# Half of the first modulation slabs multiplied by TensorE instead of VectorE

## The chip, the cores and the metric

The kernel runs on one core of a Trainium2 chip. The metric is the device time of one execution in microseconds; the kernel before takes 1960.63 us, the median of three runs from 1959.63 to 1964.99. All work is in float32. Matrix products that carry the weight are made of three products of split operands (high and low parts), but the products of this change are plain float32.

## The reference

Two transformer blocks in a row on a sequence of 256 positions of width 1024. The first begins with a modulation vector, which is what the change touches:

```python
c_act = jax.nn.silu(c)                       # 1 x 1024
mod = c_act @ w_ada[l] + b_ada[l]            # 1024 x 9216
sh1, sc1, g1, sh2, sc2, g2, sh3, sc3, g3 = [m[:, None, :] for m in jnp.split(mod, N_MOD, axis=-1)]
u = _modulate(_rmsnorm(h, norm_ffn1[l]), sh1, sc1)
h = h + 0.5 * g1 * _swiglu(u, w_ffn1_up[l], w_ffn1_down[l])
```

Everything after that (a gated delta mixer, a second feed-forward part, then the second block) is the same in both kernels. The first feed-forward part needs `sh1` and `sc1`, the first 2048 columns of `mod`, before its first matrix product can start.

## The kernel before, in words

All weights come through one ring of four buffers, `raw`, each of 128 partitions x 8 depth blocks x 256 columns of float32: 1 MB, a slab. SyncE issues each slab as two loads of 512 KB. The ring is governed by one counter, `raw_used`: it starts at 4, and the load of slab r waits until it has reached r + 1. Every consumer of a slab adds one when it is done, so slab r + 4 is loaded when slab r is free. `raw_full` of the buffer says that a slab has landed.

`w_ada` has 36 slabs, each of 256 columns of `mod`. Eight (`UPFRONT`) stand ahead of everything and give `sh1` and `sc1`. 14 more stand between the slabs of the first up-projection (`up1a`), 14 stand later.

A modulation slab is a product of one row with a 1024 x 256 matrix. VectorE does it in `dve_ada`: for each of the 8 depth blocks it multiplies the 128 x 256 block by the scalar `c_act` of each partition and adds it to one of two running sums (line 499 for the first two blocks, line 502 for the other six), then adds the two (line 505, which adds one to `raw_used`). What is left is a sum over the 128 partitions, which TensorE does in `pe_ada` (line 511): for each half of 128 columns the sum is the stationary operand and a column of ones streams past it, and the result is one column of bank 7. `ada_sum` counts these results (it starts at 2); VectorE may begin slab a when it has reached a + 1, because `acc` has two places in turn.

The opening is one block, in which the engines do this, in the order written:

- SyncE issues the loads up to the fifth slab behind the eight.
- ScalarE squares `h` for the first norm (line 615) and makes the high part of the first up-projection slab, `w_hi` (line 389).
- VectorE does the eight slabs, adds the bias in `dve_mod` (line 520, the row `mod`), which waits for all sums, and makes the low part, `w_lo` (line 397).
- TensorE sums the squares over the partitions in `total` (line 621), then does `pe_ada` eight times.

A barrier ends the block. Behind it the next block starts with `scale_col` (line 672), the norm, and the up-projection, in which every pair of columns takes one slab of `w_ffn1_up` and, up to pair 14, one of `w_ada`.

Of the kernel before, what the change touches and what calls it, by code (L numbers as in the profile page):

```python
# [23 lines left out]
P = 128  # L24
# [10 lines left out]
SLAB_K = 8  # L35
SLAB_N = 256
RING = 4
LANDED = 32
# [11 lines left out]
def at(i, step, base):  # L50

    return base if i is None else i * step + base
# [125 lines left out]
def build(nc, t, const_np, place):  # L178
    with ExitStack() as ctx:
        def sb(name, shape, dt=F32, c=ctx):  # L180
            return c.enter_context(nc.sbuf_tensor(name, shape, dt))
# [3 lines left out]
        def sem(name):  # L185
            s = nc.alloc_semaphore(name=name)
            stage_sems.append(s)
            return s
# [18 lines left out]
        raw = sb("raw", [P, RING, SLAB_K, SLAB_N])  # L207
# [11 lines left out]
        c_act = sb("c_act", [P, DT])  # L219
        banks = [ctx.enter_context(nc.psum_tensor(f"bank{i}", [P, 512], F32)) for i in range(8)]  # L220

        def const(name, rows=P):
            a, b = place[name]
            return cst[0:rows, a:b]
# [9 lines left out]
        def col(name, i, n=1):  # L234
            v, row = vcol[name]
            return vec[:, v, row + i:row + i + n]


        raw_full = [sem(f"raw_full{i}") for i in range(RING)]
        raw_used = sem("raw_used")  # L240
# [5 lines left out]
        ada_step = sem("ada_step")  # L246
        ada_sum = sem("ada_sum")
# [3 lines left out]
        def link(eng, who, ins):  # L251

            steps[who] += 1
            ins.then_inc(step[who], 1)
            eng.wait_ge(step[who], steps[who])
# [27 lines left out]
        UPFRONT, BESIDE_UP = 8, 14  # L283
# [48 lines left out]
        def load_to(sp, end):  # L332


            end = min(end, len(plan.raw))
            r = issued[0]
            while r < end:
                def rate(lap):

                    out = []  # L340
                    for u in range(RING):
                        a, b = plan.raw[r + lap * RING + u], plan.raw[r + (lap + 1) * RING + u]
                        if a[0] is not b[0] or a[2] != b[2]:
                            return None
                        out.append(b[1] - a[1])
                    return out
                laps, first = 1, rate(0) if r + 2 * RING <= end else None
                if first:
                    while r + (laps + 1) * RING <= end and rate(laps - 1) == first:
                        laps += 1  # L350
                if first and laps >= 2:
                    with sp.Fori(0, laps, 1) as i:
                        for u in range(RING):
                            sec, n, g = plan.raw[r + u]

                            sp.wait_ge(raw_used, i * RING + (r + u + 1))
                            load(sp, r + u, sec, i * first[u] + n, g)
                    r += laps * RING
                else:
                    sec, n, g = plan.raw[r]  # L360
                    sp.wait_ge(raw_used, r + 1)
                    load(sp, r, sec, n, g)
                    r += 1
            issued[0] = max(end, issued[0])

        def numbers(sec, i, U, u, g):

            k = u * sec.g + g
            r, s = sec.r0 + k * sec.rs, sec.s0 + k
            return (at(i, U * sec.g * sec.rs, r), r, at(i, U * sec.g, s), s,  # L370
                    at(i, LANDED * U * sec.g * sec.rs // RING, LANDED * (r // RING + 1)))
# [19 lines left out]
        def split_lo(dve, nxt):  # L391
            if nxt is None:
                return
            sec, g, (r, r_at, s, s_at, landed) = nxt
            kt = sec.kts[g]
            dve.wait_ge(hi_done, s + 1)
            nc.vector.tensor_tensor(w_lo[:, s_at % 2, 0:kt], raw[:, r_at % RING, 0:kt],  # L397
                                    w_hi[:, s_at % 2, 0:kt].bitcast(F32), ALU.subtract).then_inc(raw_used, 1)
# [84 lines left out]
        acc = sb("acc", [P, 3, SLAB_N])  # L483
        ADA_STEPS = SLAB_K

        def dve_ada(dve, a, a_at, r, r_at, landed, k0=0, k1=SLAB_K):

            if k0 == 0:  # L490
                dve.wait_ge(raw_full[r_at % RING], landed)
                dve.wait_ge(ada_sum, a + 1)
            for k in range(k0, k1):
                src, w = raw[:, r_at % RING, k], c_act[:, k:k + 1]
                part = acc[:, 2 if k % 2 else a_at % 2]
                if k == 1:
                    dve.wait_ge(raw_used, r + RING)
                if k < 2:
                    nc.vector.tensor_scalar(part, src, w, None, ALU.mult).then_inc(ada_step, 1)
                else:  # L500
                    dve.wait_ge(ada_step, a * ADA_STEPS + (k - 1))
                    nc.vector.scalar_tensor_tensor(out=part, in0=src, scalar=w, in1=part, op0=ALU.mult, op1=ALU.add).then_inc(ada_step, 1)  # L502
            if k1 == SLAB_K:
                dve.wait_ge(ada_step, a * ADA_STEPS + ADA_STEPS)
                nc.vector.tensor_tensor(acc[:, a_at % 2], acc[:, a_at % 2], acc[:, 2], ALU.add).then_inc(raw_used, 1)

        def pe_ada(pe, r, a, a_at, col0):

            pe.wait_ge(raw_used, r + 1 + RING)
            for j in range(2):  # L510
                mm = nc.tensor.matmul(banks[7][:, col0 + j:col0 + j + 1] if isinstance(col0, int)
                                      else banks[7][:, bass.ds(col0 + j, 1)],
                                      acc[:, a_at % 2, j * P:(j + 1) * P], const("ones")[:, 0:1],
                                      start=True, stop=True)
            mm.then_inc(ada_sum, 1)

        def dve_mod(dve, a, b, sums):

            dve.wait_ge(ada_sum, sums + 2)
            link(dve, "dve", nc.vector.tensor_tensor(mod[:, a:b], banks[7][:, a:b], col("b_ada", a, b - a), ALU.add))  # L520
# [4 lines left out]
        start = ExitStack()  # L525
# [3 lines left out]
        with nc.Block() as block:  # L529
            @block.sync  # L530
            def _(sp):
                sp.dma_start(cst[:], t["const"]).then_inc(loaded[0], 16)
                for v, group in enumerate(VECTORS):
                    row = 0
                    for name, rows in group:
                        src = t[name]
                        src = (src.rearrange("a (r p) -> (a r) p", p=P) if len(src.shape) == 2 else
                               src.rearrange("(r p) -> r p", p=P) if len(src.shape) == 1 else
                               src.rearrange("a b (r p) -> (a b r) p", p=P) if src.shape[-1] % P == 0 else
                               src.rearrange("a (r b) p -> (a r) (b p)", b=2))  # L540
                        sp.dma_start(rows_v[row:row + rows, v], src).then_inc(loaded[1 + v], 16)
                        row += rows
                load_to(sp, RING)
# [138 lines left out]
        with nc.Block() as block:  # L682
            @block.sync
            def _(sp):
                load_to(sp, S["up1a"].r0 + 1 + RING)

            @block.scalar
            def _(act):
                for u in range(4):
                    norm_ffn1.square(act, u, sq0)  # L690
                split_hi(act, (S["up1a"], 0, numbers(S["up1a"], None, 0, 0, 0)))

            @block.vector
            def _(dve):
                for a in range(UPFRONT):
                    dve_ada(dve, a, a, a, a, LANDED * (a // RING + 1))
                dve_mod(dve, 0, 2 * UPFRONT, UPFRONT)
                split_lo(dve, (S["up1a"], 0, numbers(S["up1a"], None, 0, 0, 0)))

            @block.tensor  # L700
            def _(pe):
                for u in range(4):
                    norm_ffn1.total(pe, u, sq0)
                for a in range(UPFRONT):
                    pe_ada(pe, a, a, a, 2 * a)
        first_sq.close()

        p_zero, p_ready, p_done, xu_ready, x_done, yu_ready, y_done = (
# [5 lines left out]
        def swiglu(ups, down, gate, norm, then):  # L714
# [7 lines left out]
            with ExitStack() as c:  # L722
# [6 lines left out]
                with nc.Block() as block:  # L729
# [32 lines left out]
                    def _(dve):  # L762
# [3 lines left out]
                        def between(i, u, U):  # L766
                            a = at(i, U, u + UPFRONT)
                            r_at = ups[0].r0 + 2 * u + 1
                            landed = at(i, LANDED * 2 * U // RING, LANDED * (r_at // RING + 1))
                            dve_ada(dve, a, u + UPFRONT, at(i, 2 * U, r_at), r_at, landed)  # L770
# [1302 lines left out]
        a = {n: sem("a_" + n) for n in names}  # L2073
# [296 lines left out]
```

## Time and profile before

| | |
|---|---|
| median of three runs | 1960.63 us (1959.63 to 1964.99) |
| the profiled execution, its span | 1960.6 us |
| TensorE busy | 1681.0 us, 86% |
| VectorE busy | 1136.0 us, 58% |
| ScalarE busy | 756.5 us, 39% |
| read from HBM | 249.99 MB |

The span is from the first to the last instruction of the profiled execution, and there is nothing around it that the runs' times would add: it stands at their median. The shares are means over stages with different limits. The opening that the change touches is the first 50 us of the span. TensorE's rows come in pairs, a weight load (PEld) and a matmul (PE), which overlap; the granted clock (PEclk) is 1.00 at 2.4 GHz and 0.50 at 1.2 GHz.

### The profile page before, as it was taken

The page shows a single profiled execution, that of the slowest core. Times are in us where ns is not written, and L with a number is a line of the kernel's source. Part 1 is how long each engine was busy: PE and PEld are TensorE (multiplying, and loading weights), DVE is VectorE, ACT ScalarE, POOL GpSimd, SP SyncE. Part 2 cuts the span into 40 slices and gives each one's busy share as a digit, 9 for nine tenths or more (in the row PEclk, how much of TensorE's full clock was granted, in tenths as well). Part 3 has the DMA queues.
Part 4 walks back from the last instruction along what each step waited for, and adds up shares of the span by engine and source line. Part 5 has one row for each costly group of instructions (what it writes and reads, how often), then busy time and mean ns, then how long its engine had stood idle before and what let it go on. Part 6 is the DMA issues. An engine that isn't in the chain of part 4 may idle for free. (4 is left out here: it accounts for less than half of the span.)

```text
span 1960.6 us, 36564 instructions
## 1 busy us (share of the span) xinstructions
PE 1681.0 (86%) x15063; PEld 1586.5 (81%) x15063; DVE 1136.0 (58%) x1885; ACT 756.5 (39%) x1040; POOL 108.2 (6%) x139
## 2 busy tenths in 40 slices
PE   3899989958888988999886886789997979779997
PEld 3899989927878987999885774689997956579997
DVE  6895457968795555444466554554335358554334
ACT  1554345731003634554344000356433434446432
POOL 0011000002120000110000210000000020000000
PEclk7899989958999998999987985889998985789998
DMA  9897545402234354665451000245452510225451
GB/s 301 235 315 221 178 133 171 150 0 88 87 97 122 120 182 129 173 192 178 124 161 43 2 2 7 86 129 173 162 170 97 172 50 1 86 87 171 157 170 39
DMA packets 297020, 252.88 MB, mean 129 GB/s; under 512 B 9032, under 2 KB 295597, under 8 KB 296893
## 3 DMA queue, kind: packets, MB, share of 16 engines
q1 hardware_dynamic: 296589, 249.96, 41.2%
q8 instruction: 94, 1.54, 0.3%
q10 hardware_dynamic: 304, 1.11, 0.1%
q14 instruction: 33, 0.27, 0.0%
HBM read 249.99 MB, written 1.05 MB: 128 GB/s over the span
## 5 line engine op out<-in xcount | busy, mean ns | idle before, releaser
L397 DVE TENSOR_TENSOR w_lo<-raw,w_hi 128x2048 fp32r<-128x2048 f32 (+2 forms) x203 | 456.4, 2250 | 549.6 <-ACT w_hi L389 549.3
L464 PE MATMUL bank<-x_hi,w_hi 128*128 128x256 f32 (+1 forms) x2224 | 651.6, 293 | 71.9 <-DVE x_lo L658 41.6
L466 PE MATMUL bank<-x_hi,w_lo 128*128 128x256 f32 (+1 forms) x2224 | 642.6, 289 | 0.0
L465 PE MATMUL bank<-x_lo,w_hi 128*128 128x256 f32 (+1 forms) x2224 | 642.5, 289 | 0.0
L389 ACT ACTIVATE w_hi<-raw 128x2048 fp32r<-128x2048 f32 (+2 forms) x203 | 381.6, 1880 | 470.5 <-PE bank L466 432.9
L464 PEld LDWEIGHTS bank<-x_hi,w_hi 128*128 128x128 f32 x2224 | 428.6, 193 | 81.1 <-issue 68.3
L466 PEld LDWEIGHTS bank<-x_hi,w_lo 128*128 128x128 f32 x2224 | 430.0, 193 | 0.0
L465 PEld LDWEIGHTS bank<-x_lo,w_hi 128*128 128x128 f32 x2224 | 428.9, 193 | 0.9 <-issue 0.7
L464 PE MATMUL bank<-mh_hi,w_hi 128*128 128x272 f32 x512 | 150.5, 294 | 6.6 <-PEq L2014 6.6
L466 PE MATMUL bank<-mh_hi,w_lo 128*128 128x272 f32 x512 | 149.4, 292 | 0.0
L465 PE MATMUL bank<-mh_lo,w_hi 128*128 128x272 f32 x512 | 149.1, 291 | 0.0
L464 PEld LDWEIGHTS bank<-mh_hi,w_hi 128*128 128x128 f32 x512 | 97.8, 191 | 7.2 <-issue 7.0
L464 PE MATMUL bank<-hid_hi,w_hi 128*128 128x256 f32 x352 | 100.2, 285 | 0.4 <-DVE w_lo L397 0.4
L466 PE MATMUL bank<-hid_hi,w_lo 128*128 128x256 f32 x352 | 99.0, 281 | 0.0
L465 PE MATMUL bank<-hid_lo,w_hi 128*128 128x256 f32 x352 | 99.0, 281 | 0.0
L465 PEld LDWEIGHTS bank<-mh_lo,w_hi 128*128 128x128 f32 x512 | 97.9, 191 | 0.2
L466 PEld LDWEIGHTS bank<-mh_hi,w_lo 128*128 128x128 f32 x512 | 97.8, 191 | 0.0
L502 DVE SCALAR_TENSOR_TENSOR acc<-raw,c_act,acc 128x256 f32<-128x256 f32 x216 | 96.7, 504 | 0.1
L621 PE MATMUL bank<-sq,cst 128*128 128x272 f32 (+1 forms) x160 | 51.4, 467 | 21.8 <-ACT sq L615 21.8
L464 PEld LDWEIGHTS bank<-hid_hi,w_hi 128*128 128x128 f32 x352 | 66.3, 188 | 1.1 <-issue 0.8
L465 PEld LDWEIGHTS bank<-hid_lo,w_hi 128*128 128x128 f32 x352 | 66.3, 188 | 0.1
L466 PEld LDWEIGHTS bank<-hid_hi,w_lo 128*128 128x128 f32 x352 | 66.2, 188 | 0.0
(427 smaller groups left out, 2206.9 us busy)
## 6 DMA issues: line engine op xcount, KB each, us to landing
raw<-in_mlp_w SPq DMA_DIRECT2D x128, 512.0 KB, 4.3
raw<-in_w_ffn_up SPq DMA_DIRECT2D x88, 512.0 KB, 5.2
raw<-in_w_ada SPq DMA_DIRECT2D x72, 512.0 KB, 4.7
raw<-in_w_in SPq DMA_DIRECT2D x60, 512.0 KB, 4.6
raw<-in_w_ffn_down SPq DMA_DIRECT2D x32, 512.0 KB, 4.4
raw<-in_od_w_in SPq DMA_DIRECT2D x24, 512.0 KB, 4.4
raw<-in_ev_w_in SPq DMA_DIRECT2D x18, 512.0 KB, 4.6
raw<-in_w_ffn_down SPq DMA_DIRECT2D x16, 384.0 KB, 3.8
```

The costliest lines, as they stand in the source:

```text
L389: nc.scalar.activation(w_hi[:, s_at % 2, 0:kt], raw[:, r_at % RING, 0:kt], ACT.Copy).then_inc(hi_done, 1)
L397: nc.vector.tensor_tensor(w_lo[:, s_at % 2, 0:kt], raw[:, r_at % RING, 0:kt], w_hi[:, s_at % 2, 0:kt].bitcast(F32), ALU.subtract).then_inc ...
L464: nc.tensor.matmul(out, hi, xh[:, k0 + k, 0:L], start=start, stop=False)
L465: nc.tensor.matmul(out, hi, xl[:, k0 + k, 0:L], start=False, stop=False)
L466: mm = nc.tensor.matmul(out, lo, xh[:, k0 + k, 0:L], start=False, stop=stop)
L502: nc.vector.scalar_tensor_tensor(out=part, in0=src, scalar=w, in1=part, op0=ALU.mult, op1=ALU.add).then_inc(ada_step, 1)
L621: mm = nc.tensor.matmul(banks[6][:, 0:self.L], const("ones"), sq[:, k], start=k == 0, stop=k == DT - 1)
```

## The change

Of the eight slabs ahead, those with even numbers (0, 2, 4, 6) stay as they are. Those with odd numbers go to TensorE whole, in a new function, `pe_ada_whole`: for each half of 128 columns it runs over the 8 depth blocks, with the 128 x 128 weight block from `raw` as the stationary operand and one column of `c_act` streamed past it, and accumulates in one column of bank 7. That is 16 float32 matmuls for a slab.

TensorE's order is slab 1 whole, the sum of slab 0, slab 3 whole, the sum of slab 2, and so on. VectorE's order is slab 0, 2, 4, 6. As the ring's counter has to rise in the order of the slabs, VectorE adds the one for the odd slab: in the middle of the next even slab, before its seventh depth block, it waits until TensorE has summed both slabs before (`ada_sum` at a + 2), adds one to `raw_used`, and goes on. For slab 7 it does so after `mod`.

```diff
-        def dve_ada(dve, a, a_at, r, r_at, landed, k0=0, k1=SLAB_K):
+        def dve_ada(dve, a, a_at, r, r_at, landed, k0=0, k1=SLAB_K, since=0):
...
-                    dve.wait_ge(raw_used, r + RING)
+                    dve.wait_ge(raw_used, r + RING - since)
...
+        def pe_ada_whole(pe, r, landed, col0):
+
+            pe.wait_ge(raw_full[r % RING], landed)
+            for j in range(2):
+                for k in range(SLAB_K):
+                    mm = nc.tensor.matmul(banks[7][:, col0 + j:col0 + j + 1], raw[:, r % RING, k, j * P:(j + 1) * P], c_act[:, k:k + 1],
+                                          start=k == 0, stop=k == SLAB_K - 1)
+            mm.then_inc(ada_sum, 1)
...
             def _(dve):
-                for a in range(UPFRONT):
-                    dve_ada(dve, a, a, a, a, LANDED * (a // RING + 1))
+                for a in range(0, UPFRONT, 2):
+                    landed = LANDED * (a // RING + 1)
+                    if a:
+                        dve_ada(dve, a, a // 2, a, a, landed, 0, SLAB_K - 2, since=1)
+                        dve.wait_ge(ada_sum, a + 2)
+                        dve.sem_inc(raw_used, 1)
+                        dve_ada(dve, a, a // 2, a, a, landed, SLAB_K - 2, SLAB_K)
+                    else:
+                        dve_ada(dve, a, 0, a, a, landed)
+                    dve.sem_inc(ada_step, ADA_STEPS)
                 dve_mod(dve, 0, 2 * UPFRONT, UPFRONT)
+                dve.sem_inc(raw_used, 1)
                 split_lo(dve, (S["up1a"], 0, numbers(S["up1a"], None, 0, 0, 0)))
...
             def _(pe):
...
-                for a in range(UPFRONT):
-                    pe_ada(pe, a, a, a, 2 * a)
+                for a in range(0, UPFRONT, 2):
+                    pe_ada_whole(pe, a + 1, LANDED * ((a + 1) // RING + 1), 2 * a + 2)
+                    pe_ada(pe, a, a, a // 2, 2 * a)
```

The order of TensorE's instructions behind the norm's total, before the change; each row is an instruction of the program, with its output and inputs and what it waits for:

```order
L621 MATMUL bank6<-sq0,cst 128x256
L511 MATMUL bank7<-cst,acc 128x1 [waits raw_used]
L511 MATMUL bank7<-cst,acc 128x1
L511 MATMUL bank7<-cst,acc 128x1 [waits raw_used]
L511 MATMUL bank7<-cst,acc 128x1
L511 MATMUL bank7<-cst,acc 128x1 [waits raw_used]
L511 MATMUL bank7<-cst,acc 128x1
```

The same place of the changed kernel:

```order
L630 MATMUL bank6<-sq0,cst 128x256
L522 MATMUL bank7<-c_act,raw 128x1 [waits raw_full1]
L522 MATMUL bank7<-c_act,raw 128x1 x15
L511 MATMUL bank7<-cst,acc 128x1 [waits raw_used]
L511 MATMUL bank7<-cst,acc 128x1
L522 MATMUL bank7<-c_act,raw 128x1 [waits raw_full3]
L522 MATMUL bank7<-c_act,raw 128x1 x15
L511 MATMUL bank7<-cst,acc 128x1 [waits raw_used]
```

The two sums of a slab that VectorE made remain for every second slab, and ahead of them stand 16 matmuls that wait for a landed slab and not for VectorE.

VectorE's order before the change, from the second slab on:

```order
L499 TENSOR_SCALAR acc<-raw,c_act 128x256 [waits ada_sum,raw_full1]
L499 TENSOR_SCALAR acc<-raw,c_act 128x256 [waits raw_used]
L502 SCALAR_TENSOR_TENSOR acc<-raw,c_act,acc 128x256 [waits ada_step] x6
L505 TENSOR_TENSOR acc<-acc 128x256 [waits ada_step]
L499 TENSOR_SCALAR acc<-raw,c_act 128x256 [waits ada_sum,raw_full2]
```

The same place of the changed kernel, up to the start of slab 4:

```order
L499 TENSOR_SCALAR acc<-raw,c_act 128x256 [waits ada_sum,raw_full2]
L499 TENSOR_SCALAR acc<-raw,c_act 128x256 [waits raw_used]
L502 SCALAR_TENSOR_TENSOR acc<-raw,c_act,acc 128x256 [waits ada_step] x4
L502 SCALAR_TENSOR_TENSOR acc<-raw,c_act,acc 128x256 [waits ada_sum,ada_step]
L502 SCALAR_TENSOR_TENSOR acc<-raw,c_act,acc 128x256 [waits ada_step]
L505 TENSOR_TENSOR acc<-acc 128x256 [waits ada_step]
L499 TENSOR_SCALAR acc<-raw,c_act 128x256 [waits ada_sum,raw_full0]
```

Slabs 1, 3, 5 and 7 are gone from VectorE, and each slab left has a second wait for `ada_sum` in its middle.

## Rows read from the trace of the kernel before

**Rows 1.** Who waited for whom, 17 to 46.3 us: total, times, longest.
```profile
PE bank L511 <- DVE acc L505: 15.1, 6, 3.2
...
DVE mod L520 <- PE bank L511: 1.1, 1, 1.1
DVE acc L499 <- PE bank L511: 0.6, 1, 0.6
```

**Rows 2.** Timeline of VectorE and ScalarE: start, duration, instruction, [idle before, releaser].
```profile
17.09 0.62 DVE L499 TENSOR_SCALAR acc<-raw,c_act 128x256 f32<-128x256 f32 x2 [0.41 <-PEq L529]
17.62 2.46 DVE L502 SCALAR_TENSOR_TENSOR acc<-raw,c_act,acc 128x256 f32<-128x256 f32 x6
20.11 0.42 DVE L505 TENSOR_TENSOR acc<-acc 128x256 f32<-128x256 f32 x1
20.45 0.61 DVE L499 TENSOR_SCALAR acc<-raw,c_act 128x256 f32<-128x256 f32 x2
...
40.79 1.91 ACT L389 ACTIVATE w_hi<-raw 128x2048 fp32r<-128x2048 f32 x1 [21.62 <-DMA raw<-in_w_ffn_up]
44.51 0.42 DVE L505 TENSOR_TENSOR acc<-acc 128x256 f32<-128x256 f32 x1
46.04 0.17 DVE L520 TENSOR_TENSOR mod<-bank,vec 128x16 f32<-128x16 f32 x1 [1.10 <-PE bank L511]
46.24 2.29 DVE L397 TENSOR_TENSOR w_lo<-raw,w_hi 128x2048 fp32r<-128x2048 f32 x1
50.10 0.17 DVE L672 SCALAR_TENSOR_TENSOR scale_col<-mod,vec 128x8 f32<-128x8 f32 x1 [1.56 <-PEq L682]
```

**Rows 3.** TensorE: timeline from 17 us, then line 511's count and ns (min/median/max).
```profile
17.66 6.42 PE L621 MATMUL bank<-sq,cst 128*128 128x256 f32 x16 [1.31 <-ACT sq L615]
...
23.70 1.08 PEld L511 LDWEIGHTS bank<-cst,acc 128*128 128x128 f32 x8
...
L511 PE MATMUL bank<-cst,acc x4: 352/352/372, 28.0 to 28.7; 128*128 128x1 f32 x4
...
L511 PE MATMUL bank<-cst,acc x144: 166/250/373, 23.9 to 599.0; 128*128 128x1 f32 x144
```

**Rows 4.** Timeline of the weight loads of a run with 8 columns each.
```profile
400.25 0.55 PEld L1045 LDWEIGHTS bank<-g_log,cst 128*128 128x128 f32 x2
400.69 0.55 PEld L1044 LDWEIGHTS bank<-g_log,cst 128*128 128x128 f32 x2
...
402.82 0.55 PEld L1045 LDWEIGHTS bank<-g_log,cst 128*128 128x128 f32 x2
```

**Rows 5.** Timeline of the matmuls of a run with 32 columns each.
```profile
383.11 0.18 PE L985 MATMUL bank<-w_ba_hi,x_hi 128*128 128x32 f32 x1
...
384.03 0.26 PE L985 MATMUL bank<-w_ba_hi,x_hi 128*128 128x32 f32 x1
...
388.05 0.26 PE L985 MATMUL bank<-w_ba_hi,x_hi 128*128 128x32 f32 x1
...
388.50 0.63 PE L988 MATMUL bank<-heads_row,cst 1*128 1x32 f32 x2
```

**Rows 6.** Stretches: length, busy of PE, PEld, DVE, ACT, POOL, PEclk, DMA share, GB/s.
```profile
17.00:20.00 3.00, 2.34 (x6) 1.89 (x7) 2.91 (x8) 2.17 (x4) 0.00 (x0) 1.00 1.10 347
...
23.00:26.00 3.00, 1.86 (x13) 1.67 (x11) 2.34 (x8) 0.00 (x0) 0.00 (x0) 1.00 1.00 311
26.00:27.00 1.00, 0.00 (x0) 0.00 (x0) 1.00 (x3) 0.00 (x0) 0.00 (x0) 0.78 1.09 379
27.00:30.00 3.00, 1.01 (x4) 0.93 (x4) 2.96 (x9) 0.00 (x0) 0.00 (x0) 0.50 0.72 222
...
381.60:385.00 3.40, 3.40 (x33) 3.40 (x31) 3.40 (x9) 1.58 (x5) 0.00 (x0) 1.00 0.00 0
385.00:388.30 3.30, 3.30 (x32) 3.30 (x31) 3.27 (x9) 0.63 (x1) 0.00 (x0) 1.00 0.01 2
388.40:391.80 3.40, 0.73 (x4) 0.56 (x3) 1.23 (x1) 3.37 (x8) 0.00 (x0) 0.50 0.00 0
```

**Rows 7.** Loads of line 330: at 24.3 us, from 20 to 50, the first eight.
```profile
L330 SPq DMA_DIRECT2D raw<-in_w_ada x1: 508/508/508, 24.3 to 24.3; - x1
DMA to landing us min/median/max: 4.8/4.8/4.8
...
L330 SPq DMA_DIRECT2D raw<-in_w_ada x12: 367/435/509, 20.6 to 45.4; - x12
DMA to landing us min/median/max: 3.4/4.4/5.6
...
L330 SPq DMA_DIRECT2D raw<-in_w_ada x8: 409/510/1859, 8.6 to 14.2; - x8
DMA to landing us min/median/max: 3.6/7.5/9.2
```

**Rows 8.** The stretch behind the barrier, same columns as rows 6.
```profile
50.00:145.00 95.00, 84.55 (x670) 83.79 (x671) 89.23 (x162) 54.24 (x58) 8.34 (x11) 0.93 0.98 275
```

## The prediction, on record before the changed kernel ran

> **What bounds the kernel now.** I read first the two-engine picture of the opening (who waited for whom from 17 to 46 us), then the timelines of VectorE and TensorE there, then the clock by stretches, then the loads, and last the stage behind the barrier. The opening is a chain on VectorE. TensorE waits for VectorE's sum six times, 15.1 us in all, and VectorE, once started, waits for TensorE only twice, 0.6 us at the third slab and 1.1 us at the very end [rows 1]. A slab costs VectorE two products, six multiply-adds and an addition; the next slab's first row comes 3.36 us later (17.09 to 20.45) [rows 2]. Eight slabs and the 0.6 us wait take it from 17.09 to the add at 44.51; then TensorE sums the last slab and VectorE reads the result at 46.04 [rows 2]. Behind that stand w_lo (46.24, 2.29 us), SyncE's last load issue and the barrier, and the next stage opens with scale_col at 50.10 [rows 2]. So whatever moves the row at 46.04 moves the barrier, provided that what stands between stays in its place.
>
> TensorE does little: 16 records of the norm's total from 17.66, then the slab sums, 4 records each [rows 3]. A float32 matmul leaves two records: line 511 has 144 for 36 slabs of two matmuls [rows 3].
>
> **What the change removes.** VectorE loses slabs 1, 3, 5 and 7: 4 x 3.36 = 13.4 us. That would be the gain if VectorE alone set the end.
>
> **What it adds.** For each of those slabs TensorE gets 16 float32 matmuls, 8 depth blocks for each of two column halves: 32 records, each a load of a 128x128 weight block with one column streamed after it. The ones-matmuls of the four others stay, 4 records each. After the norm's total TensorE thus has 4 x (32 + 4) = 144 records before VectorE can read bank 7, where it had 32.
>
> What does one cost? The form with `raw` as the stationary operand is not in the trace, but the cost of a record with few columns is there in a long row. Sixteen such pairs with 8 moving columns start at 400.25, ..., 402.82, that is 12 records in 2.57 us: 0.2138 us each, at a granted clock of 0.50, the level of 1.2 GHz [rows 4]. At 1.00, the level of 2.4 GHz, stands a run of 48 records with 32 columns, of which line 985 has every third: from its row at 384.03 to that at 388.05 are 36 records in 4.02 us, 0.112 us each [rows 5]. Neither has one column, but 8 or 32; the 8 one-column records of line 511 at the upper level took 1.08 us, of which the last load is 0.19, so 7 steps in 0.89 us, the pace of the 32-column run but for 0.1 us at the first, behind the wide matmul before it [rows 3, 5]. So 0.112 and 0.214 are my two ends, one for each clock. A serial end (each load of a pair waiting for the matmul before it, 0.33 and 0.35 us by the durations of line 511 at the lower level) is excluded by the same 12 records, which stand closer than that [rows 3, 4].
>
> So the clock decides. At 23.70, where the new matmuls begin, it is at the upper level; it reads 1.00 from 23 to 26, 0.78 from 26 to 27 and 0.50 from 27 on, so it falls at 26.56 [rows 6]. In that stretch TensorE did the end of the total and 8 one-column records, then nothing. Will 144 one-column records back to back hold the clock? The run of lines 985 to 987 answers: TensorE was busy without a pause from 381.6 to 388.3, from 383.11 on with records of 32 columns, and the clock was down to 0.50 right behind it, while line 988 still ran from 388.50 [rows 5, 6]. A run of such records did not keep the upper level, and I expect no more of one column than of 32. I take 1.2 GHz from 26.56 on.
>
> The Trainium skill, "TensorE: Matmul & The Clock Gate", section "Why this matters for your kernels", says to keep TensorE continuously busy and it will have the full clock. By that rule the new stream would run at 2.4 GHz; the row at 388 us speaks against it, since an engine busy without a pause lost the clock. It comes back as a rival below.
>
> **The sum.** TensorE starts at 23.70. Up to 26.56 it gets (26.56 - 23.70 - 0.10) / 0.112 = 25 records done. The other 119 take 119 x 0.2138 = 25.4 us, to 52.0, and the last one ends 0.3 us after the next would start: 52.3. VectorE's mod follows within 0.05 us: 52.3 against 46.04, **+6.3 us**.
>
> Does TensorE wait in between? The new order makes each engine wait for the other: VectorE starts slab a only when TensorE's slab a - 1 is summed (`ada_sum`), and all that is queued behind on VectorE waits too. It then needs 3.4 us, while TensorE has 4 + 32 records before it wants that result: 36 x 0.214 = 7.7 us. VectorE is early by 4 us, so the 13.4 us it saves become idle time.
>
> Loads: slab 5 is issued when VectorE, in the middle of slab 2, frees the buffer of slab 1. Slab 1 is done at 28.4 (25 fast and 7 slow records), six of VectorE's eight steps take some 2.2 us (two products 0.53, four of six multiply-adds in 2.46) [rows 2], so the issue is at 30.6. A load is two issues, 0.4 us apart, with 3.4 to 5.6 us to landing, median 4.4; the second half of slab 5, issued at 24.3, took 4.8 [rows 7]. So 0.4 + 4.8 us, to 35.8. TensorE wants it after 72 records: 26.56 + 47 x 0.2138 = 36.6. Slab 7, by the same count, lands at 43.4 and is wanted after 108 records, at 44.3. Both are hidden, with 0.8 us to spare, none if the landing takes 5.6. The first slab of the next stage is released at about 39.5, lands by 46.5, and ScalarE's split of it (1.91 us) is ready before 52.3 [rows 2].
>
> Behind mod the order is as before: the release of slab 7's buffer moves to after mod, so the second load from the last goes out some 7 us later than now; it is wanted only in the second pair of the next stage, where the last load, released by w_lo as now, is just as late. I give it nothing. Is the delay swallowed later? From 50 to 145 us VectorE is busy 89.23 of 95 us and the DMA engines 0.98, both driven by releases behind the barrier [rows 8]: nothing there runs on a clock of its own. The delay stays whole.
>
> The profiled execution has a span of 1960.6 us, the median of the three runs is 1960.63: 1960.6 + 6.3 = **1966.9 us**, 0.32% more. About 0.3%, 5.9 us, is what a measurement of this kernel tells from no change, so the forecast stands just past that line.
>
> **Rivals.**
> (a) The full clock holds. For it: in the run from 383.11 it stayed up for some 5 us, and here it fell only after TensorE had stood still; against it: it did fall at the end of that run [rows 5, 6]. The page named above would have it so. Then a TensorE slab costs 32 x 0.112 = 3.6 us and the loads decide. VectorE starts slab 2 at 27.6, slab 5 is issued at 29.8 and lands at 35.0; slab 6, freed at 31.1, lands at 38.0 (3.0 us for a slab of 1.05 MB at the 347 GB/s of 17 to 20 us) [rows 6]; slab 7, freed by 34, follows at 41.0. TensorE: 41.0 + 3.6 + 0.45 + 0.3 = 45.3, against 46.04: -0.7, 1959.9 us. Not slower; it decides from a clock of 1.00 past 27 us. 7%.
> (b) The clock stays up longer, but not to the end. For it: the 5 us that it lasted from 383.11, where it has 2.9 here past 23.70 [rows 5, 6]. Against: ahead of that run stood wide matmuls without a gap, ahead of this one the total, whose end here did not keep it past 26.56. If it is up for twice the 2.9 us, the second 2.9 us do 5.8 us of slow work: 1964.0. 13%.
> (c) A load shows. Issue to landing reached 9.2 us in the first burst, when eight were queued at once [rows 7]; with it slabs 5 and 7 would come 3.6 us too late each. Halfway, +3.5 us: 1970.4. The two loads have no eight ahead of them. 8%.
> (d) VectorE's 13.4 us come through: 1947. The semaphore order and TensorE's 144 records exclude it but for a mistake of mine. 1%.
>
> **How the numbers follow.** Forecast 71%: 1966.9, by itself 1965.5 to 1968.5 (the place of the fall in the clock and the runs' own spread). For 8 in 10 I leave out (a), (d), the far end of (c) and the tails: 1962 to 1971.5. Slower by over 0.3% means above 1966.5: two thirds of the forecast's 71% and all of (c), 0.55. Faster by over 0.3% is (d) and what I can't see, 0.04. The rest, 0.41, is within.
>
> **What would show it.** Line 522 with 128 records, 0.214 us apart after the first 25; the granted clock 0.50 from about 27 to past 60; VectorE idle 4 us before each slab, released by TensorE; mod at 52.3; scale_col at 56.4; and from there the same rows as now, 6.3 us later. Wrong it would be by a clock of 1.00 in the opening, by TensorE waiting for `raw`, or by a pace other than 0.214.

## The result, and the profile after

Five runs of each kernel on one chip: after 1969.96 us median (1964.13 to 1981.01), before 1959.63 us (1957.91 to 1964.99); ratio 1.0048, 95% interval 1.0025 to 1.0072. The change makes the kernel slower, by 10.3 us from median to median where 6.3 were forecast. The forecast of 1966.9 us is 3.1 us below the median and lies inside the interval (1964.5 to 1973.7 us). The profiled execution of the changed kernel has a span of 1966.9 us and was timed at 1968.75: some 1.8 us lie around the span, in every run. Two executions among all that follow, of 2212 and 2965 us, showed a far lower clock than the rest (0.70 and 0.74) and are left out of every comparison.

Who waited for whom in the opening, 17 to 60 us (total, times, longest), after; before it was TensorE that waited, 15.1 us [rows 1]:

```profile
DVE acc L499 <- PE bank L522: 11.5, 3, 4.4
DVE mod L529 <- PE bank L511: 5.0, 1, 5.0
```

The wait has changed sides, and nothing waits for a load of `raw`. The timeline of VectorE, after, for [rows 2]:

```profile
16.95 0.62 DVE L499 TENSOR_SCALAR acc<-raw,c_act 128x256 f32<-128x256 f32 x2 [0.41 <-PEq L538]
24.83 0.61 DVE L499 TENSOR_SCALAR acc<-raw,c_act 128x256 f32<-128x256 f32 x2 [4.43 <-PE bank L522]
31.16 0.62 DVE L499 TENSOR_SCALAR acc<-raw,c_act 128x256 f32<-128x256 f32 x2 [2.88 <-PE bank L522]
38.84 0.62 DVE L499 TENSOR_SCALAR acc<-raw,c_act 128x256 f32<-128x256 f32 x2 [4.23 <-PE bank L522]
47.29 0.17 DVE L529 TENSOR_TENSOR mod<-bank,vec 128x16 f32<-128x16 f32 x1 [5.00 <-PE bank L511]
47.61 2.29 DVE L397 TENSOR_TENSOR w_lo<-raw,w_hi 128x2048 fp32r<-128x2048 f32 x1
51.47 0.17 DVE L681 SCALAR_TENSOR_TENSOR scale_col<-mod,vec 128x8 f32<-128x8 f32 x1 [1.57 <-PEq L691]
```

The four slabs that VectorE lost are idle time. But mod comes at 47.29, where 52.3 was predicted: 1.25 us late, not 6.3. TensorE's own timeline, for [rows 3], says why:

```profile
17.53 3.72 PE L630 MATMUL bank<-sq,cst 128*128 128x256 f32 x16 [1.31 <-ACT sq L624]
21.09 3.63 PE L522 MATMUL bank<-c_act,raw 128*128 128x1 f32 x32
24.57 0.58 PE L511 MATMUL bank<-cst,acc 128*128 128x1 f32 x4
25.02 6.02 PE L522 MATMUL bank<-c_act,raw 128*128 128x1 f32 x32
...
31.75 6.96 PE L522 MATMUL bank<-c_act,raw 128*128 128x1 f32 x32
...
39.44 6.96 PE L522 MATMUL bank<-c_act,raw 128*128 128x1 f32 x32
```

The norm's total took 3.72 us here and 6.42 before [rows 3], so the new matmuls began at 21.09, not at 23.70. Stretches of the opening, after (columns as in [rows 6]):

```profile
20.00:23.00 3.00, 3.00 (x24) 2.86 (x23) 0.40 (x1) 0.00 (x0) 0.00 (x0) 1.00 1.10 348
23.00:26.00 3.00, 3.00 (x29) 3.00 (x29) 1.17 (x4) 0.00 (x0) 0.00 (x0) 1.00 0.80 252
26.00:27.00 1.00, 1.00 (x7) 1.00 (x7) 1.00 (x4) 0.00 (x0) 0.00 (x0) 0.54 0.00 0
27.00:30.00 3.00, 3.00 (x15) 3.00 (x16) 1.24 (x4) 0.00 (x0) 0.00 (x0) 0.50 0.79 269
30.00:40.00 10.00, 10.00 (x48) 10.00 (x48) 4.58 (x13) 0.00 (x0) 0.00 (x0) 0.50 1.09 323
```

The clock falls at 26.08 (0.54 = 0.50 + 0.08 x 0.50) while TensorE is busy without a pause, as forecast. Up to there go (26.08 - 21.09) / 0.112 = 45 records and not 25; the other 99 take 99 x 0.2133 = 21.1 us, to 47.2, where mod stands.

Where, then, did the span's 6.3 us come from? Compared row by row, VectorE is 1.25 us late at 47 us, on a par at 97 us, and 1.7 us ahead at 997 us. The loss lies between 1080 and 1148 us, in the stage of the chunks, which the change does not touch: VectorE is 8.7 us late behind it, gets 4.0 of them back by 1188 us, and ends 6.3 us late. Its first rows on VectorE, before and then after:

```profile
1088.60 1.29 DVE L1751 TENSOR_TENSOR ak_t<-bank,cst 128x512 f32<-128x512 f32 x2 [8.62 <-PE bank L1729]
...
1136.33 1.29 DVE L1751 TENSOR_TENSOR ak_t<-bank,cst 128x512 f32<-128x512 f32 x2 [6.51 <-PE bank L1729]
```

```profile
1089.73 1.29 DVE L1770 TENSOR_TENSOR ak_t<-bank,cst 128x512 f32<-128x512 f32 x2 [10.99 <-PE bank L1748]
...
1142.54 1.29 DVE L1770 TENSOR_TENSOR ak_t<-bank,cst 128x512 f32<-128x512 f32 x2 [9.62 <-PE bank L1748]
```

VectorE waits 2.4 and 3.1 us longer for the same matmuls. The granted clock (before the last two numbers), again before and after:

```profile
1080.00:1088.00 8.00, 6.93 (x66) 6.65 (x67) 0.00 (x0) 1.08 (x2) 1.94 (x3) 0.79 0.00 0
1088.00:1092.00 4.00, 3.96 (x64) 3.63 (x64) 2.16 (x4) 0.00 (x0) 0.00 (x0) 1.00 0.02 6
```

```profile
1080.00:1088.00 8.00, 8.00 (x62) 7.66 (x62) 0.00 (x0) 1.09 (x2) 1.02 (x2) 0.55 0.01 3
1088.00:1092.00 4.00, 4.00 (x32) 3.66 (x31) 1.29 (x2) 0.00 (x0) 0.00 (x0) 0.50 0.00 0
```

Half the records in the same 4 us, at half the clock. So the first pair of traces agrees with my number by luck, along a path that I had not predicted. What is the change's own share, and what is the clock's play? That is what the experiments are for.

### The profile page after: what moved, and what is told of

The parts are those of the page before. It is cut to its first block and busy times, and to the rows that moved or that the text cites. A ratio compares the mean times of both kernels' runs of the same rounds, so it can differ in the third digit from the quotient of the medians.

```text
span 1966.9 us, 36755 instructions
## 1 busy us (share of the span) xinstructions
PE 1705.0 (87%) x15175; PEld 1609.8 (82%) x15175; DVE 1123.0 (57%) x1849; ACT 756.4 (38%) x1040; POOL 107.7 (5%) x139
## 5 line engine op out<-in xcount | busy, mean ns | idle before, releaser
L502 DVE SCALAR_TENSOR_TENSOR acc<-raw,c_act,acc 128x256 f32<-128x256 f32 x192 | 86.9, 508 | 0.1
L630 PE MATMUL bank<-sq,cst 128*128 128x272 f32 (+1 forms) x160 | 49.4, 452 | 21.8 <-ACT sq L624 21.8
```

The source lines that it names most:

```text
L630: mm = nc.tensor.matmul(banks[6][:, 0:self.L], const("ones"), sq[:, k], start=k == 0, stop=k == DT - 1)
```

## The experiments

**1. The same two kernels again** (no edit), to see what differs between executions of one program.

> The changed kernel once more, unchanged, in five rounds, for a second trace and five more times. Theory A (the opening's delay is all there is): the row mod stands between 47 and 53 us, and every later row is late by the same amount up to the end; the ratio is 1.003. Theory B (the opening's delay is one part, and the rest is where TensorE's granted clock changes in later stages): mod stands anywhere between 47 and 53 us, the end is late by another amount than mod is, and the difference arises in stages behind 440 us in which the clock column differs from that of the kernel before; the ratio is 1.003 to 1.006 with a wide spread of the single times.

> The kernel before, unchanged, under its own name, for a second trace and its own spread. Both theories: mod at 46.0 us, a ratio of 1.000. Theory A: all rows agree within 1 us with the first trace up to the end. Theory B: the end moves by several us between two traces of one and the same program, in stages in which the granted clock differs, and the first 60 us agree within 0.5 us, as VectorE sets them.

After again: 1972.02 us median of 12, ratio 1.0034 (1.0014 to 1.0054). Before again: 1961.77 us median of 12, ratio 1.0006 (0.9989 to 1.0023). In the trace of the changed kernel the opening now went as predicted; TensorE and then VectorE:

```profile
18.18 6.75 PE L630 MATMUL bank<-sq,cst 128*128 128x256 f32 x16 [1.31 <-ACT sq L624]
24.77 4.10 PE L522 MATMUL bank<-c_act,raw 128*128 128x1 f32 x32
...
29.58 6.96 PE L522 MATMUL bank<-c_act,raw 128*128 128x1 f32 x32
...
52.79 0.17 DVE L529 TENSOR_TENSOR mod<-bank,vec 128x16 f32<-128x16 f32 x1 [5.01 <-PE bank L511]
```

The total took the long form, and mod stands at 52.79. TensorE's total started 0.52 us later than in the first trace of before (18.18 against 17.66), which leaves +6.2: the sum of the prediction (+6.1 against the trace of before_again, 46.72). The unchanged kernel's second trace has the slow form of the chunk stage, with the same waits as the first trace of after:

```profile
1087.71 1.29 DVE L1751 TENSOR_TENSOR ak_t<-bank,cst 128x512 f32<-128x512 f32 x2 [10.99 <-PE bank L1729]
...
1140.55 1.29 DVE L1751 TENSOR_TENSOR ak_t<-bank,cst 128x512 f32<-128x512 f32 x2 [9.63 <-PE bank L1729]
```

So that loss is not the change's alone. Theory A, by which all rows shift alike, falls: before_again opens 0.7 us later than the first trace of before (0.5 was expected at most) and ends 4.3 us later; after_again is 6.1 us behind before_again at mod, 10.2 at 500 us and 10.4 at the end. Both are as theory B had it.

**2. Five more traces of the two kernels** (no edit; the last with timed runs).

> The changed kernel once more, for its trace. Theory (the opening costs by TensorE's pace and by where the clock rises and falls): mod's row comes 6 us later than in a trace of the kernel before that opened alike (51.5 to 53) if the total runs at the lower clock until past 23 us, and only 1 to 2 us later (47 to 48) if it runs at the upper one from the start; nothing between but by a fall of the clock at another time. Theory on the rest (the clock between 1075 and 1150 us is drawn anew in each execution, for either kernel): the distance between the first ak_t of the two chunk groups is one of 47.7, 49.7, 52.8 or 55.0 us, as in the nine traces so far. Rival (the later start pushes that stage into the lower clock each time): 52.8 or 55.0 again, as in both traces of this kernel so far.

> The kernel before once more, for its trace. Theory: mod within 1 us of 46.0 to 46.8, wherever the clock rises, since VectorE's chain sets it; the distance between the two first ak_t is one of 47.7, 49.7, 52.8 or 55.0 us (47.7 and 52.8 in its two traces so far). Rival (that the later start of the changed kernel's stage is what slows it there): 47.7 or 49.7 here.

> As the run with the changed kernel above: mod at 51.5 to 53 or at 47 to 48 by where the clock rises; ak_t distance any of 47.7, 49.7, 52.8, 55.0 us by the theory that it is drawn anew, 52.8 or 55.0 by the rival.

> As the run with the kernel before above: mod at 46.0 to 46.8; ak_t distance any of 47.7, 49.7, 52.8, 55.0 us by the theory, 47.7 or 49.7 by the rival.

> The changed kernel once more with the kernel before beside it, for the size of the mean difference. The openings of the traces so far put mod 1.3 to 2.0 us later than before where the norm's total ran at the upper clock (two of four) and 5.4 to 6.3 us later where it did not (the other two), so about 3.7 us on average, 0.19%: the theory that the rest is drawn alike for both kernels expects a ratio between 1.001 and 1.003. The rival, that the later start also makes the stage at 1088 us slower (its four traces had 52.8 or 55.0 us between the first ak_t rows there, the kernel before had 47.7 once, 52.8 once, 55.0 twice), adds up to 2 us: 1.003 to 1.005, and no 47.7 in the trace of this run either.

All nine traces, in us. "ak_t to ak_t" is the distance between the two rows shown above.

| trace | the total's 16 records | mod | ak_t to ak_t | span |
|---|---|---|---|---|
| before, 1st | 6.42 | 46.04 | 47.73 | 1960.6 |
| before_again | 6.65 | 46.72 | 52.84 | 1964.9 |
| before_c | 3.72 | 45.54 | 55.00 | 1970.8 |
| before_d | 6.34 | 46.36 | 55.02 | 1971.0 |
| after, 1st | 3.72 | 47.29 | 52.81 | 1966.9 |
| after_again | 6.75 | 52.79 | 55.02 | 1975.4 |
| after_c | 3.72 | 47.51 | 55.01 | 1970.7 |
| after_d | 5.41 | 51.80 | 55.00 | 1974.1 |
| after_e | 3.72 | 47.50 | 52.86 | 1967.3 |

The opening: before moves by 1.2 us whatever the total does, since VectorE's chain sets it. After comes in two sizes, 47.3 to 47.5 after a fast total and 51.8 to 52.8 after a slow one. Against before with a total of the same form, after costs +1.75 to +2.0 us (47.29 to 47.51 against 45.54) or +6.1 to +6.8 (52.79 against 46.04 to 46.72). As the total starts anywhere from 17.53 to 18.34 us, it is cleaner to count from its start: +2.1 us with a fast total in all three traces of after, +6.0 to +6.3 with a slow one. The forecast had seen the second only. The 5.41 of after_d is a third form, with no partner among the traces of before: there the clock reads 0.50 from 19.5 to 23.0 us, and mod comes 4.9 to 5.2 us later than behind a slow total of before, counted in the same way.

What tells the two forms apart is where the clock rises. In the first trace of before the total's records start 0.427 us apart up to 23.15 us and 0.216 us apart behind it; in the first of after they are 0.216 us apart from the second on. The view of stretches reads 1.00 from 17 to 23 us in both, but it also does so where the trace holds no clock record at all. The first record, a rise to 1.00, stands at 23.2 to 24.3 us in the four traces with a slow total, and at 15.8 to 16.3 us in the five others. So the slow total ran at the lower pace up to the rise.

The chunk stage: 55.0 stands twice in four traces of before, so the rival that the later start alone causes it falls. 47.7 stands in none of five traces of after; whether that is chance these traces can't say. A late start does not rule the short form out, though: it is there (47.8) in experiment 6, where mod comes at 61.14.

The times: after_e gave 1971.21 us, ratio 1.0025 (1.0004 to 1.0046); the point lies in the range of the theory, the interval covers the rival's too. All single times together: 31 of after have mean 1971.2 and lowest 1962.1, 94 of before mean 1963.8 and lowest 1957.6. The difference is +7.4 us, by resampling of the single runs 5.4 to 9.4. The chips differ and not all sets have as many runs of each kernel; within the four sets that have both, the means differ by 11.0, 8.1, 5.0 and 4.6 us, weighted +7.1 (5.1 to 9.1). The openings of the table differ by only 49.4 - 46.2 = 3.2 us in the mean.

**3. The delay alone:** the kernel before, with mod in its place and 14 additions on VectorE behind it.

```
                 dve_mod(dve, 0, 2 * UPFRONT, UPFRONT)
+                for _n in range(14):
+                    link(dve, "dve", nc.vector.tensor_tensor(acc[:, 2], acc[:, 0], acc[:, 1], ALU.add))
                 split_lo(dve, ...)
```

> The kernel before with 14 additions of VectorE put between mod and w_lo, each waiting for the one before: a bare delay of some 6.4 us at the place where the change delays, with nothing given to TensorE. Theory A: +6.4 us at the end, ratio 1.0033, and the shift of VectorE's rows constant behind 60 us. Theory B: a mean of +6.4 us, with single times spread over 10 us and more. A third view (the delay is swallowed in the first up-projection, where VectorE waits for loads now and then): the shift falls below 3 us by 150 us, and the ratio is under 1.0015.

1971.87 us median of 12, ratio 1.0051 (1.0035 to 1.0067). VectorE:

```profile
46.75 0.17 DVE L520 TENSOR_TENSOR mod<-bank,vec 128x16 f32<-128x16 f32 x1 [1.11 <-PE bank L511]
46.96 6.41 DVE L699 TENSOR_TENSOR acc<-acc 128x256 f32<-128x256 f32 x14
53.40 2.29 DVE L397 TENSOR_TENSOR w_lo<-raw,w_hi 128x2048 fp32r<-128x2048 f32 x1
57.25 0.17 DVE L672 SCALAR_TENSOR_TENSOR scale_col<-mod,vec 128x8 f32<-128x8 f32 x1 [1.56 <-PEq L682]
```

The delay is 6.4 us, and this trace's opening is another 0.7 us late by itself: w_lo is 7.2 us later than in [rows 2]. The rows stay 5.1 to 7.4 us late up to 1000 us, and the span ends 7.8 us later (the chunk stage took 49.7 us here, 2.0 more than in that trace of before). The lowest time is 7.0 us above the lowest of before (1964.66, 1957.61), and the ratio's interval is +6.9 to +13.1 us: nothing of the delay is swallowed. The step "the delay stays whole" is shown, with no TensorE work added: the view that the first up-projection swallows it is out. The ratio, about +10 us, lies above the bare delay, and no run says why.

**4. The wide form:** the operands of the four TensorE slabs exchanged, so that 256 columns of `raw` move past one column of `c_act`. ScalarE copies the row out, and two matmuls turn it into columns. VectorE's waits change too: it frees the odd buffer as soon as the row is summed, and no longer waits for that slab before it begins the next. So this is more than an exchange of operands. The central line of the edit:

```
-                    mm = nc.tensor.matmul(banks[7][:, col0 + j:col0 + j + 1], raw[:, r % RING, k, j * P:(j + 1) * P], c_act[:, k:k + 1], ...
+                mm = nc.tensor.matmul(banks[4 + n % 2][0:1, 0:SLAB_N], c_act[:, k:k + 1], raw[:, r % RING, k], ...
```

> The changed kernel with the two operands of TensorE's product exchanged for slabs 1, 3, 5 and 7: c_act is the stationary block (one column) and 256 columns of raw stream past it, 8 matmuls a slab; ScalarE copies the row out and two one-row matmuls turn it into columns of bank 7. VectorE frees the odd buffer as soon as the row is summed and no longer waits for it to begin. Theory A and B alike, if wide columns keep the clock at 1.00: 16 records of 0.217 us a slab, 3.5 us in place of 6.8, TensorE waits for loads from slab 5 on, and mod stands at about 40 us, 6 us earlier than before the change; the ratio 0.997 by A, 0.996 to 0.999 by B. If the clock falls anyway, a record takes 0.43 us, a slab 6.8, and mod is at 50 to 52 us.

1965.34 us median of 12, ratio 1.0013 (0.9996 to 1.0029). TensorE, SyncE and VectorE:

```profile
20.88 3.61 PE L523 MATMUL bank<-raw,c_act 128*1 128x256 f32 x16
...
35.56 2.26 SPq L330 DMA_DIRECT2D raw<-in_w_ada  x2
37.12 6.46 PE L523 MATMUL bank<-raw,c_act 128*1 128x256 f32 x16 [2.83 <-DMA raw<-in_w_ada]
...
45.22 0.17 DVE L543 TENSOR_TENSOR mod<-bank,vec 128x16 f32<-128x16 f32 x1 [7.71 <-PE bank L531]
```

A slab takes 3.61 us. The stretches, of which the third to last number is the clock:

```profile
23.00:26.00 3.00, 3.00 (x16) 1.36 (x15) 1.30 (x3) 0.37 (x1) 0.00 (x0) 1.00 0.89 269
...
30.00:36.00 6.00, 4.29 (x23) 2.13 (x21) 2.00 (x7) 0.37 (x1) 0.00 (x0) 1.00 1.10 352
36.00:40.00 4.00, 2.88 (x7) 0.85 (x8) 1.48 (x4) 0.00 (x0) 0.00 (x0) 0.51 1.17 305
```

The clock held, 1.00 from 17 to 36 us. Then the last slab was not there: TensorE stood still 2.83 us, the clock fell at 36.1 us, and the slab took 6.46 us. mod stands at 45.22, where about 40 was expected, and the expected gain (ratio 0.997) did not come. Once the stream is fast, the loads set the end. This run was the first to show it, and my own expectation had missed it.

**5. Half of the stream:** the second four of the eight depth blocks are left out on TensorE (so its four slabs sum half the depth).

```
-                for k in range(SLAB_K):
+                for k in range(SLAB_K // 2):
```

> The changed kernel, in which TensorE multiplies only four of the eight depth blocks of slabs 1, 3, 5 and 7 (the other four are left out of the result): 16 records a slab in place of 32, all waits as they are. Theory A (TensorE's stream of one-column records at the lower clock sets the opening): 64 records fewer on the path, up to 13.7 us; the loads come in before that: slab 5 issued at 28, slab 7 landing at 38 to 38.5, mod at 42 to 43 us, 10 us earlier than where the stream runs late and 3.5 us earlier than before the change. The alternative (the waits between VectorE and TensorE set it, whatever the stream's length): mod stays at 47 us or later.

1964.15 us median of nine, ratio 1.0003 (0.9982 to 1.0023). TensorE, SyncE and VectorE:

```profile
32.12 3.58 PE L522 MATMUL bank<-c_act,raw 128*128 128x1 f32 x16 [2.12 <-DMA raw<-in_w_ada]
...
39.71 3.57 PE L522 MATMUL bank<-c_act,raw 128*128 128x1 f32 x16 [3.16 <-DMA raw<-in_w_ada]
...
44.17 0.17 DVE L529 TENSOR_TENSOR mod<-bank,vec 128x16 f32<-128x16 f32 x1 [4.91 <-PE bank L511]
44.43 2.64 SPq L330 DMA_DIRECT2D raw<-in_w_ada  x2
...
47.51 2.43 SPq L330 DMA_DIRECT2D raw<-in_w_ffn_up  x2
50.48 0.17 DVE L681 SCALAR_TENSOR_TENSOR scale_col<-mod,vec 128x8 f32<-128x8 f32 x1 [3.00 <-PEq L691]
```

With 64 of the 128 records gone the slowdown is gone: the records' count and pace are the cause. But no gain takes its place. TensorE now waits 2.1 and 3.2 us for loads, mod misses the expected 42 to 43 us, and though it is 1.9 us early against [rows 2], the barrier is not: SyncE's last load issue takes 2.43 us, where two issues take 0.99 in after, and scale_col stands at 50.48. In before, after, wide, half_depth and mix alike, scale_col starts 0.55 us after SyncE's last load issue ends, and that issue starts as soon as w_lo has ended.

**6. Wide fillers:** four 256-column float32 matmuls in each TensorE slab, so that every fifth record is wide.

```
                 for k in range(SLAB_K):
+                    if k % 4 == 0:
+                        nc.tensor.matmul(banks[5][:, 0:T1], const("ones"), sq0[:, k], start=True, stop=True)
```

> The changed kernel with four wide matmuls more in each of the slabs 1, 3, 5 and 7 (the ones block against 256 columns of the squares, into a bank nobody reads), put among the one-column ones: 8 records of 0.217 us more a slab at the upper clock. If wide columns hold the clock: granted clock 1.00 past 40 us, one-column records at 0.112 us, a slab 5.3 us in place of 6.8 in spite of the added work, and mod at 44.5 to 47.5 us. If it is the gaps or something else that takes the clock down: 0.50 from 27 us on, a slab 10.2 us, and mod at 63 to 67 us.

One run, 1979.04 us, span 1977.3. Two stretches:

```profile
26.00:27.00 1.00, 1.00 (x10) 1.00 (x9) 0.00 (x0) 0.00 (x0) 0.00 (x0) 0.75 0.00 0
27.00:30.00 3.00, 3.00 (x13) 2.82 (x14) 2.92 (x8) 0.00 (x0) 0.00 (x0) 0.50 0.08 13
```

The clock fell at 26.5 all the same. That some wide records among the narrow ones would hold it was my guess, and it failed; slabs of wide records held it (experiment 4, and experiment 7, whose clock reads 1.00 from 22.0 to 39.1 us). mod came at 61.14, 15.1 us late (earlier than the 63 to 67 expected, since the total was of the fast form), and the span ended 16.7 us later: a delay twice as long is kept too, in one pair of traces that both drew the fast form of the chunk stage (waits of 8.63 and 6.51 here).

**7. A better split:** the wide form for slabs 1, 3 and 5, VectorE for the other five (edit as in 4, with `ada_step` given back for three slabs only).

> The kernel with exchanged operands, with slab 7 back on VectorE: TensorE multiplies 1, 3 and 5, VectorE 0, 2, 4, 6 and 7. The wait for the load of slab 7 no longer has TensorE standing still ahead of a whole slab at the lower clock. Slab 6 lands at 34, slab 7 at 37; VectorE does 6 from 34.1 and 7 from 37.5 to 40.9, and mod stands at 42 us, 4 us earlier than before the change, whatever the clock. If the gain is kept: ratio 0.998. The alternative (a delay or gain of the opening doesn't reach the end one to one, since loads and clock decide later): 1.000.

1963.73 us median of 12, ratio 1.0005 (0.9990 to 1.0021). SyncE and VectorE:

```profile
42.53 3.60 SPq L330 DMA_DIRECT2D raw<-in_w_ada  x2
43.61 0.17 DVE L543 TENSOR_TENSOR mod<-bank,vec 128x16 f32<-128x16 f32 x1 [1.11 <-PE bank L511]
...
46.65 2.36 SPq L330 DMA_DIRECT2D raw<-in_w_ffn_up  x2
49.56 0.17 DVE L695 SCALAR_TENSOR_TENSOR scale_col<-mod,vec 128x8 f32<-128x8 f32 x1 [2.93 <-PEq L706]
```

mod is 2.4 us early (4 were expected) and scale_col only 0.5: SyncE, whose last issue stands before the barrier, gives the rest back, and no gain shows in the times (0.998 was expected if it was kept). No version that I ran is shown to beat the kernel before.

## Why the prediction was right, and where it was not

- **A slab on VectorE is worth nothing, since TensorE takes the chain over.** Right: VectorE idles 4.23 us before each slab in the slow stretch (4 predicted).
- **144 records at 0.112 and 0.214.** Right: 36 records take 3.93 us at the upper level (21.09 to 25.02, 0.109 each) and 7.69 us at the lower (31.75 to 39.44, 0.2136 each). The price of another form of record, 8 or 32 columns, carried over to one column [rows 4, 5].
- **The clock falls although TensorE is busy.** Right: at 26.1 to 27.8 us in all five traces of after, and at 26.5 in experiment 6. In the four traces of before, where TensorE stood still but for the slab sums, it fell at 26.5 to 27.5: the narrow stream did no better than a pause. The Trainium skill, "TensorE: Matmul & The Clock Gate", section "Why this matters for your kernels", says to keep TensorE continuously busy for the highest throughput; the fall at 26.08 with TensorE busy 3.00 of 3.00 us on either side disagrees for one-column records, and experiment 4 agrees for wide ones (busy 3.00 of 3.00 us from 23 to 26, clock 1.00 up to 36).
- **The start at 23.70.** Here the step failed: I read TensorE's start and pace from one trace, as if the total's 6.42 us belonged to the kernel. It is 3.72 us in four of nine traces, in which the clock rises before the total and not near its end. There rival (b), a clock up for longer, came in by its other end: up earlier, not down later. The change costs about 2 us there, and about 6 where the total is slow. That the forecast of one form alone came near the measured time of a mixture of both is in part luck. (A smaller term: the last record ends 0.14 us after the next would start, not 0.3.)
- **The loads are hidden with 0.8 us to spare.** Right that they are hidden; the margin goes with the form. In the first trace of after slab 5 landed 0.4 us before TensorE reached it (31.36, 31.75), in after_again 1.8 us before (35.45, 37.26). What stood just behind them I had not seen: a faster stream runs into the loads at once (experiments 4 and 5). My price for rival (a), slab 7 at 41.0 and mod at 45.3, came near what experiment 4 gave (45.22) by luck: there the slab came at 37.1 and the clock fell.
- **The delay stays whole.** Shown by experiment 3 for a bare delay. In single pairs of traces it is drowned: after_c against before_c is 2.0 us late at mod, 2.5 at 284 us, 0.3 at 604 us and -0.1 at the end; after_again against before_again goes from +6.1 to +10.4.
- **Nothing around the span.** Wrong by about 1.8 us: the profiled execution of before would be timed at 1962.4, not at the median of 1960.63. The forecast does not suffer, since its 6.3 us stand on the median as well.
- **Open:** the mean difference, +7.4 us (5.4 to 9.4; set by set +7.1, 5.1 to 9.1), is above the 3.2 us by which the openings of the traces differ, and around the 6.3 predicted. Either the timed runs open slowly more often than the nine traced ones, or a late opening makes later stages draw the lower clock more often. Experiment 3, whose ratio too stands above its bare delay, is compatible with the second; nothing here decides it.

## What to carry to other kernels

Moving work from a busy engine to an idle one pays only if the idle one's chain, at the pace of the clock that it will really have, is shorter: here VectorE's 3.36 us a slab became 7.7 us of one-column float32 records at 0.2136 us, and the saved time turned into idle time. Before giving a load-fed chain a faster engine, compare it with the rate at which its slabs land, and look at what the issuing engine then does in front of the next barrier. And look at several traces of the kernel before: a duration in one of them may be one of two.

## What the runs showed of the hardware that I had not expected

- The clock column can read 1.00 where the trace holds no clock record. From 17 to 23 us it does so in every trace but one of the nine, yet the same 16 records took 3.72 us in four traces of the two kernels, with the first record of the clock at 15.8 to 16.3 us, and 6.3 to 6.8 us in four others, with the first at 23.2 to 24.3. The distance of the records, 0.216 or 0.427 us, is the better witness.
- The same stage, untouched, takes 47.7, 49.7 (in experiment 3), 52.8 or 55.0 us between two of its rows from one execution to the next, with the granted clock at 0.50 or at 1.00 in it. That alone is 7.3 us, more than the 6.3 us forecast for the change, and about half of the 15.2 us over which before's single times spread (1957.6 to 1972.8).
- A run of one-column float32 records, busy in 3.00 of 3.00 us, lost the clock; so did one with every fifth record of 256 columns; slabs of 256-column records, with a few narrow ones between two slabs, kept it from 17 to 36 us. Wide records lost it once too: in after_d it fell at 19.5 us, 1.2 us into the total, which TensorE had begun at 18.34 after 1.84 us of waiting.
- One load's issue on SyncE takes 0.37 to 0.58 us where at most two earlier loads have not landed, and 1.2 to 2.8 us where five have not, in every trace here; with three or four it is either. So the issuing engine is held, and with it the barrier behind it: two issues take up to 3.6 us in experiments 4, 5 and 7, in place of 0.9 to 1.0.
